# An attention stage on one NeuronCore: the first sliding-window item is scored ahead of the first FoX tile, and two sets of helper writes move on VectorE

## What is computed

```python
u = rmsnorm(h, g_pre)
qa, ka, va, za, qf, kf, vf, zf, ff, ga, gf = split(u @ w_in)
# sliding branch: 8 query heads, 2 key heads, block of 128 queries,
# keys = 16 meta tokens + 64 or 128 before + 128 of the block
logits = einsum(q, k) * ATTN_SCALE + bias          # bias = -slope * distance, or NEG_INF
probs = softmax(concatenate([logits, sink]))[..., :-1]
y_swa = einsum(probs, v) * silu(za)
# FoX branch: 8 heads, causal over all tokens, with forget gates
c_key = cumsum(log_sigmoid(ff + b_forget))
logits = einsum(q, k) * ATTN_SCALE + (c[t] - c_key[s])   # masked to s <= t
y_fox = (softmax(logits) @ v) * silu(zf)
merged = (sigmoid(ga + b_gate[0]) * (y_swa @ w_up_swa)
          + sigmoid(gf + b_gate[1]) * (y_fox @ w_up_fox))
h = h + rmsnorm(merged @ w_out, g_post)
```

## Time and profile before

| | us |
|---|---|
| median of three runs | 829.82 |
| lowest and highest | 829.27, 831.76 |
| the profiled execution | 829.26 |
| its span, first to last instruction | 827.5 |
| TensorE busy in the span | 797.1 |
| VectorE, GpSimd, ScalarE busy | 495.0, 336.6, 315.6 |

### The profile page before, as it was taken

The page is one execution under the profiler, slowest core; times in us unless marked ns, Lnnn a source line. Parts: engine busy times, 40 slices in busy tenths (PEclk is TensorE's granted clock), DMA queues, the critical chain, the costliest instruction groups (busy, mean ns, idle before and its releaser), DMA issues.

```text
span 827.5 us, 12903 instructions
## 1 busy us (share of the span) xinstructions
PE 797.1 (96%) x4514; PEld 644.2 (78%) x4514; DVE 495.0 (60%) x1060; ACT 315.6 (38%) x648; POOL 336.6 (41%) x287
## 2 busy tenths in 40 slices
PE   4999999999999999999999998999998999999997
PEld 3999999987878878788787865666664788878885
DVE  6834878356676767645546356777778744442222
ACT  6531241333334333333333336666777223232111
POOL 1112314444445434444443414756785344512221
PEclk9999999999999999999999999999999999999999
DMA  9442424569957346356363599999900575352221
GB/s 298 112 121 53 130 65 131 128 164 263 243 169 200 99 143 193 98 162 177 102 179 98 137 245 241 245 242 216 214 1 2 169 212 152 102 192 89 97 82 76
DMA packets 122712, 125.00 MB, mean 151 GB/s; under 512 B 30116, under 2 KB 92404, under 8 KB 122648
## 3 DMA queue, kind: packets, MB, share of 16 engines
q1 hardware_dynamic: 121208, 119.92, 54.1%
q10 hardware_dynamic: 1440, 4.26, 1.4%
HBM read 90.93 MB, written 34.92 MB: 152 GB/s over the span
## 4 chain that ended last, share of the span: by engine, by line
PE 77%; issue 7%; POOL 6%; DVE 5%; ACT 3%; DMA 2%; SPq 0%; DVEq 0%; ACTq 0%; POOLq 0%
PE PS L1881 19%; PE PS L1882 19%; PE PS L1883 19%; POOL acc L1239 4%; PE PS L2130 4%; PE PS L2132 4%; PE PS L2131 3%; PE PS L1988 2%; DVE t_val L1619 2%; POOL probs L1215 1%; PE PS L2053 1%; POOL w_plain L1191 1%; ACT p_fox L1392 1%; DMA QB<-max_dram 1%; PE PS L1903 1%
## 5 line engine op out<-in xcount | busy, mean ns | idle before, releaser
L1170 POOL TENSOR_TENSOR ops<-s_sum,ops 128x512 fp32r<-128x512 f32 x64 | 88.0, 1386 | 112.1 <-ACT ops L1268 112.1
L1881 PE MATMUL PS<-t_hi,ops 128*128 128x512 f32 x256 | 101.1, 395 | 0.0
L1882 PE MATMUL PS<-t_lo,ops 128*128 128x512 f32 x256 | 99.8, 390 | 0.0
L1883 PE MATMUL PS<-t_hi,ops 128*128 128x512 f32 x256 | 99.8, 390 | 0.0
L1170 POOL TENSOR_TENSOR ops<-raw,ops 128x512 fp32r<-128x512 f32 x48 | 65.5, 1365 | 67.6 <-ACT ops L1268 67.4
L1191 POOL TENSOR_TENSOR w_plain<-raw,w_plain 128x1024 fp32r<-128x1024 f32 x10 | 27.9, 2792 | 102.0 <-ACT w_plain L1297 102.0
L1698 DVE TENSOR_TENSOR z_tmp<-u,PS 128x512 f32<-128x512 f32 x48 | 33.0, 687 | 49.1 <-PE PS L1883 28.2
L1239 POOL TENSOR_TENSOR acc<-acc,p_fox 128x400 f32<-128x400 f32 (+5 forms) x76 | 59.9, 808 | 5.0 <-ACT p_fox L1392 4.0
L1268 ACT ACTIVATE ops<-s_sum 128x512 fp32r<-128x512 f32 x64 | 39.6, 623 | 53.1 <-DVE s_sum L1500 42.5
L1392 ACT ACTIVATE p_fox<-PS,neg_c_col 128x512 f32<-128x512 f32 (+5 forms) x112 | 54.3, 536 | 14.0 <-PE PS L2039 9.4
L1883 PEld LDWEIGHTS PS<-t_hi,ops 128*128 128x128 f32 x256 | 48.1, 188 | 10.6
(11 more groups left out here) (204 smaller groups left out, 2160.2 us busy)
## 6 DMA issues: line engine op xcount, KB each, us to landing
raw<-in_w_in_dram SPq DMA_DIRECT2D x34, 512.0 KB, 5.3
q_dram<-stage_b SPq DMA_DIRECT2D x32, 256.0 KB, 3.0
g_dram<-stage_b SPq DMA_DIRECT2D x32, 256.0 KB, 2.0
tanh_g<-g_dram SPq DMA_DIRECT2D x16, 512.0 KB, 4.0
max_k<-k_dram SPq DMA_DIRECT2D x16, 260.0 KB, 5.3
max_c<-neg_c_dram SPq DMA_DIRECT2D x8, 520.0 KB, 6.4
x_all<-in_x_dram SPq DMA_DIRECT2D x8, 512.0 KB, 7.6
raw<-in_w_in_dram SPq DMA_DIRECT2D x16, 256.0 KB, 4.7
```

The source lines that it names most:

```text
L1170: nc.gpsimd.tensor_tensor(ops[:, i % OPS, 1], op_source(p, name), ops[:, i % OPS, 0].bitcast(F32), ALU.subtract).then_inc(op_ready, 1)
L1881: pe.matmul(dst, hi_w, hi, start=first, stop=False)
L1882: pe.matmul(dst, hi_w, lo, start=False, stop=False)
L1883: return pe.matmul(dst, lo_w, hi, start=False, stop=last)
```

## The change

Item 0 is no longer given a slot by the condition. Its `score` is put ahead of unit 0, its `exp` in unit 0, and `norm`, `trans` and `pv_swa` follow in units 1, 2 and 3. The condition for the others is worked out anew, for 31 items, so that items 1 to 8 take the units of items 0 to 7 (items 1 and 2 are scored in units 3 and 4, which were those of items 0 and 1), items 9 to 22 stand one unit sooner or where they stood, and from item 23 (unit 36) on all stand where they stood. VectorE writes the tables `far_alibi` and `far_meta` (nine instructions) after the maxima of item 0 instead of ahead of them, and the ones of `KB[1]` (two memsets) right behind them instead of in unit 4. TensorE's first score waits for the fold S4 instead of for the last one.

```diff
@@ attention_steps @@
     spread = len(units) - 8 - FIRST_SLOT
+    steps.append(score(0))
...
-        slot = u >= FIRST_SLOT and next_item < ITEMS and (u + 1 - FIRST_SLOT) * ITEMS // spread > next_item
+        slot = u >= FIRST_SLOT and next_item < ITEMS and (u + 1 - FIRST_SLOT) * (ITEMS - 1) // spread >= next_item
         if slot:
             steps.append(score(next_item))
...
-        if slot:
+        if slot or not u:
             steps.append(item("exp", next_item))
@@ VectorE @@
             for st in steps_c:
                 kind = st["kind"]
-                if kind == "load_values" and (st["j"], st["part"]) == (1, 0):
+                if kind == "exp" and st["i"] == 0:
+                    dve.wait_ge(folded, n_fold)
+                    for x in range(2):
+                        nc.vector.tensor_copy(far_alibi[:, x, N_META:], alibi[:, N_META:]).then_inc(far_ready, 1)
+                    for x in range(1, NQ):
+                        nc.vector.tensor_scalar(far_meta[:, x - 1, :], alibi[:, 0:N_META], -0.5 * P * x, None,
+                                                ALU.add).then_inc(far_ready, 1)
                     dve.wait_ge(product_done, len(prods))
                     for h, part in ((0, Q1), (1, Q0)):
                         nc.vector.memset(KB[1][part, h, :].bitcast(F32), 1.0).then_inc(halves_cleared, 1)
                 elif kind == "score":
                     i, b, a = st["i"], st["i"] % PROB_RING, st["i"] % 2
                     dve.wait_ge(ms_filled, st["ms"] + 1)
-                    if i == 0:
-                        for x in range(2):
-                            nc.vector.tensor_copy(far_alibi[:, x, N_META:], alibi[:, N_META:]).then_inc(far_ready, 1)
-                        for x in range(1, NQ):
-                            nc.vector.tensor_scalar(far_meta[:, x - 1, :], alibi[:, 0:N_META], -0.5 * P * x, None,
-                                                    ALU.add).then_inc(far_ready, 1)
+                    if i == 1:
                         dve.wait_ge(far_ready, NQ + 1)
@@ TensorE, score @@
                     if i == 0:
                         pe.wait_ge(swa_loaded, 16 * 2)
                         pe.wait_ge(halves_cleared, 3)
-                        pe.wait_ge(folded, n_fold)
+                        pe.wait_ge(folded, fold_n[N_COUPLES - 1, "S4"])
```

## The result

| | before | after |
|---|---|---|
| median, us | 829.9 | 836.8 |
| lowest, highest | 829.3, 832.2 | 835.3, 838.1 |
| runs | 6 | 6 |
| profiled execution | 829.26 | 838.06 |

The changed kernel is slower: the ratio is 1.0065 with a 95% interval of 1.0043 to 1.0088. The ratio of the two medians, 1.0083, lies within the interval. The profiled execution has a mean granted clock of 0.988 where the one before had 0.998. Sums from the traces hold for these two executions.

The account below looks back on a forecast made before the run. TensorE was taken to set the pace from unit 7 on, with idle time to win only at stage C's start. -2.84 + 6.1 = +3.3 us on 829.26 gave 832.5, as a median 833.1 us; range 830.2 to 836.0.

Parts of the forecast that it names:

- item 0's early last step: pv_swa moved from unit 6 to 3 meets unlanded loads v_b and z: waits of 2.3, 3.4 and 0.4, +6.1 us.
- the new places of items 1 and on: From unit 7 on, changed mixtures of work: new idle times as likely as old ones going, net nothing.
- What goes, -2.84 us: Start of stage C: three idle times go (2.23 us) and item 0's score (0.61) fits the wait before the first tile.
- What moves at no cost: Units 0 to 3: item 0's trans finds its input; exponentials and late additions fit, put at nothing, range 0 to 0.4 us.
- The wait for `v_b`: Item 0's pv_swa, after unit 3: TensorE arrives at 497.74, the load lands at 499.9, so it waits 2.3 us.
- The waits of 3.4 and 0.4 us: TensorE waits 3.4 us ahead of item 1's trans in unit 5, then 0.4 in unit 6, behind VectorE's stop for z.
- The landing of `z`: Load y<-z_dram, issued at 501.91, lands after 3.7 us at 505.6; VectorE stands for it some 5 us.
- rival (b): The clock falls to half in TensorE's longest pause in stage C, costing 1.25 us: 834.4 us; chance 0.12.
- Unit 7: Sign in the changed kernel's trace: unit 7 starts at about 512.4 us instead of 507.7.
- rival (a): Idle times between 529 and 588 us, 3.31 us today, take back all or part of the loss: 830.6; chance 0.22.
- rival (d): More goes wrong at the start, each further wait 0.5 to 1.2 us, up to +2.5: 835.6 us; chance 0.06.

Follow-up runs that it names:

- e3: Changed kernel, but only item 0's early score and maxima, tables and ones behind them; all other steps as before: 828.2 us, ratio 0.9954 to before.
- e1: Changed kernel with item 0's last step (pv_swa) back in unit 6, directly ahead of item 1's: 831.1 us, ratio 0.9994 to before.
- e10: Same program as e3, measured again with more rounds: 828.4 us, ratio 0.9959 to before.
- e4: Changed kernel with 14 unused matmuls filling TensorE's wait for v_b: 837.9 us, ratio 1.0061 to before.
- e5: Changed kernel with unused matmuls in both waits, 14 ahead of v_b and 13 ahead of item 1's probs: 834.8 us, ratio 1.0042 to before.
- e2: Changed kernel with the first load of z issued early, directly behind v_b: 834.0 us, ratio 1.0028 to before.
- e6: e3 with items 9 and on in the changed kernel's units, one sooner or the same: 828.9 us, ratio 0.9975 to before.
- e7: Changed kernel with the first load of z issued later, behind the two loads that followed it: 841.6 us, ratio 1.0120 to before.
- e9: Changed kernel with e1's edit, and z and the second half of the sliding queries issued behind v_b: 830.1 us, ratio 0.9991 to before.
- e8: Kernel before with only the tables and ones moved, right behind stage B's last fold; score where it stood: 828.4 us, ratio 0.9969 to before.

## Why the prediction was right, and where it was short

The direction and the mechanism were right: 833.1 us was forecast, with slower at 0.58. The measured 836.8 is 3.7 us more, and above the upper end of the range, 836.0; by the ratio, 1.0065 of 829.8, it is 835.2, inside it. By ratios the parts are: -3.8 for what e3 has of the change (forecast -2.84), +5.9 for item 0's early last step (e1; forecast 6.1), and +3.3 left for the new places of items 1 and on (with e1's waits of 0.92 and 1.02 us for loads in it), which the forecast put at nothing. That the second agrees so well is in part luck: 6.1 was a sum of waits, and the 5.9 hold the half clock as well. Point by point:

- **What goes, -2.84 us.** Right. e3 and e10 have it whole, -3.8 and -3.4.
- **What moves at no cost.** Right: item 0's `trans` found its input, and the added wait in units 1 and 2 is none; 0.30 us stands at the same place before and after.
- **The wait for `v_b`.** 2.3 us were forecast, 3.62 came, since the load took 8.8 us instead of 7.2. As said, it did not count by itself: in the changed kernel `z` was later still. But the clock fell in it.
- **The waits of 3.4 and 0.4 us.** Measured were 0.77 ahead of `trans` and none in unit 6. At half clock and after the longer wait for `v_b`, TensorE came to both later. With the first wait filled and the clock kept up (e4) they are 3.21 and 0.57, so the path was right and the clock was missing from it.
- **The landing of `z`.** The term that carried the sum, and too small. I took 505.6. Counted from the first tile it came 1.3 us later than before (16.8 less 0.1 for the release, against 15.4), not because it was slow (3.7 us both times) but because it was issued later: SyncE waits for the last stores of stage B to land, and those landed later. The load of `v_b`, in the same queue, was slower too. Both differ nearly as much between executions of one program: e3 and e10 have 7.2 and 8.6 us for `v_b`, and issue `z` 11.6 and 12.6 us after their first tile; before has 7.2 and 11.8, the changed kernel 8.8 and 13.1. Over all traces `v_b` took 8.0 to 9.1 us in the five kernels with item 0's `pv_swa` in unit 3 and 7.2 to 8.6 in the seven others. So nothing shows that the change made these landings later; the forecast took one execution's row for a fixed time.
- **The clock, rival (b).** It had 0.12 and was to cost 1.25 us. It fell in each trace that has the unfilled pause, and costs some 2.05 us before unit 7 (from e5's trace). My argument against it, that the pause ends about when the fall began at the end of the span, leant on one row; the pause for `v_b` was longer than forecast, and the clock fell within it and not behind the one for `z`. The rule that the Trainium skill gives for this (TensorE: Matmul & The Clock Gate, "HAM oscillation"), that a wait for a transfer puts the engine back to half clock, is what the trace shows in the wait of 3.62 us, where the clock fell about 3.0 us after it had begun.
- **Unit 7.** Forecast 4.7 us later, measured from the first tile 8.2 later. Of the 3.5 between them 1.3 are from `z` and 2.05 from the clock. These are the mis-sized terms.
- **The later idle times, rival (a).** The forecast put the net of these at nothing, which was wrong. Between 529 and 588 us TensorE's idle time fell from 3.31 to 1.26 us, so 2.05 us were given back; compared unit for unit, by the idle times that the timelines list from unit 7 to 34 without the new pause, it is 3.23 against 1.26. I had the items from unit 7 on at most one unit sooner; items 4 and 6 are two units sooner. But the new order made the pause of 1.69 us in unit 34 and the half clock behind it. From the three stretches there (1.5 us at 0.87, 2 at 0.50, 2 at 0.74) that is 0.2 + 1.0 + 0.5, an estimated 1.7 us lost. I took new idle times to be short ones, 0.5 to 1.2 us, under rival (d).

The whole of the profiled execution adds up: 0.7 us before the first tile, 8.2 to unit 7 less 1.46 for the one item's work more that is then already done (`score` 0.52, `trans` 0.39, `pv_swa` 0.55), -2.05, +1.69, +1.7 make 8.8; the two profiled executions are 8.80 apart.

## What to carry to other kernels

Moving a unit of work sooner moves its last step sooner as well. List every wait of every step of it, with the time at which what it waits for is there, loads above all, before valuing the room at its front. Move what wins by itself first: helper writes out of the item's chain and the first score into an existing wait gave 3.4 to 3.8 us, and pulling the whole pipeline along gave it all back and 5.4 us more.

A landing that one trace shows is one draw. Take its time from several executions before a sum rests on it; here one program's load took 7.2 us in one and 8.6 in another.

When a wait has two causes in a row, filling the first one shows which counts: the one that is over last.

## What the runs showed of the hardware that was not expected

- After a pause of TensorE of 1.69 us the granted clock can fall. It stood at 0.50 for about 3.4 us, beginning 0.6 to 1.7 us after the pause, when matmuls were running again. It fell so in the traces of the changed kernel, e1, e2, e4, e6 and e7, and not in those of e5 and e9, which have the same pause between the same instructions. That one program pays this in some executions and not in others is likely, since e9's ten runs have mean granted clocks from 0.994 to 1.000, but no program with the pause was traced twice.
- The clock that fell in the 3.62 us wait stayed at half up to 515 us, while TensorE was busy 3.00 of 3 us and then 6.23 of 7. In e2 it was back 6.0 us after the wait of 4.00 us; in the changed kernel TensorE worked for 6.2 us before its next stop, and the clock was not back.
- The same VectorE instruction, `den_row<-den_row,y` on 128x512, took 0.85 us before (at 582.93) and 1.79 in the changed kernel (at 588.64). It took 0.83 to 0.85 in before, e3, e8 and e10, and 1.79 in all eight kernels with the late shift, so these 0.94 us go with the new order and are part of the pause of 1.69. GpSimd was busy throughout the instruction in both traces; what differs is what ran there, additions on `acc` before and, for the most part, a 128x512 `up_lo<-up_raw,up_hi` after. That this is the cause was not tested.
- One load of 512 KB, `y<-z_dram`, took 3.7, 6.5 and 9.1 us to land in the changed kernel, e7 and e2, where it was issued at 503.9, 506.5 and 494.5 us, behind other loads and stores each time.
